# RWKV outputs of the first tile normalized on GpSimd during the second tile's rounds, roots and reciprocals tile by tile

## The chip, the cores and the metric

The kernel runs on one core of a Trainium2 chip. The metric is the device time of one execution in microseconds (us), median of the runs shown. The core has five engines that run their own instruction queues and meet only at semaphores: TensorE (PE; its weight loads are listed apart as PEld), VectorE (DVE), ScalarE (ACT), GpSimd (POOL) and SyncE (SP), which here only issues DMAs.

## The reference

Two transformer blocks on 256 tokens of width 2048. The change lies in the first one, in its mixer: an RWKV-7 group of 16 heads of 64 columns, whose outputs y are normalized head by head and then scaled, shifted, given a bonus and gated, and a sparse attention group that scores all keys with 16 small index heads, keeps the 64 best keys of a token and attends to them. Both halves, side by side, are the input of the product with `w_mix_out`.

```python
def rwkv7_group(p, mu, w0, w_decay_up, a0, a_up, g_up, k_k, k_a, r_k, lnx_w, lnx_b):
...
    _, y = lax.scan(step, s0, (tm(r4), tm(w4), tm(k4), tm(v4), tm(kk), tm(a4)))
    y = tm(y)
    mean = jnp.mean(y, axis=-1, keepdims=True)
    var = jnp.mean(jnp.square(y - mean), axis=-1, keepdims=True)
    yn = ((y - mean) * lax.rsqrt(var + RWKV_LN_EPS)).reshape(B, S, RWKV_WIDTH)
    yn = yn * lnx_w.astype(f32) + lnx_b.astype(f32)
    bonus = (jnp.sum(r4 * k4 * r_k.astype(f32), axis=-1, keepdims=True) * v4).reshape(B, S, RWKV_WIDTH)
    return ((yn + bonus) * g.astype(f32)).astype(p.dtype)

def dsa_group(p, pos):
...
        rel = jax.nn.relu(jnp.einsum('bqhd,bsd->bqhs', qib.astype(f32), ki))
        score = jnp.einsum('bqhs,bqh->bqs', rel, wib)
        causal = key_pos[None, :] <= q_pos[:, None]
        score = jnp.where(causal[None], score, -1e30)
        _, idx = lax.top_k(score, n_sel)
...
def first_block(...):
...
        p = rms_norm(h, norm_mix[l]) @ w_in[l]
        y_rwkv = rwkv7_group(p[..., :RWKV_COLS], ...)
        y_att = dsa_group(p[..., RWKV_COLS:], positions)
        h = h + jnp.concatenate([y_rwkv, y_att], axis=-1) @ w_mix_out[l]
...
```

## The kernel before

The 256 tokens are two tiles (`TILES`, index `t`) of 128 partitions. Products with weights run in fp32 split in a high and a low part: ScalarE rounds a slab of weights (L781), GpSimd makes its remainder (`rests`, L616), TensorE multiplies (L2014, L2024). After the input product `in` come three stages without weights, and then the product `mix`.

**RWKV rounds.** `PAIRS` holds four rounds: two for the first tile (n = 0, 1) and two for the second (n = 2, 3). A round is a chain of 16 stages between TensorE (L2142 to L2267), VectorE (L1508 to L1554) and ScalarE (L995 to L1018), for two groups `u` of four heads that alternate. A round starts with transposes (L2185) that VectorE and ScalarE copy out of PSUM (L1511, L997); then VectorE masks the products (L1514 to L1519; of these only L1517 reads two SBUF tiles, the others PSUM), and it ends with VectorE's L1552 and L1553, which write y over `key_t`. L1547, late in a round, reads two SBUF tiles too.

**Statistics and outputs of y.** GpSimd waits for both rounds of a tile (L694, L695) and makes the head means (L697, L698), the centred y (L699), its squares (L700), their head sums (L659, L661) and the variance plus epsilon (L702, which raises `s_yv`). This runs for tile 0 during round n = 2 and for tile 1 behind round n = 3. The root (ScalarE, L1034) and the reciprocal (VectorE, L1573) are taken once, for both tiles, on `yst[:, 1]`, 32 columns. Then GpSimd, from L704 on, runs the outputs of both tiles, six instructions of 128x1024 each: times the reciprocal root (L707), times and plus the gains (L708, L709), the bonus (L710), its addition (L711), the gate (L712, which raises `s_yr`). Right behind them in its queue stand the remainders of `mix` (L616), of which three can run before TensorE has used any.

**Index scores and the search.** After the rounds TensorE makes index products (L2297), ScalarE their relu (L1038), and VectorE adds sixteen of them, weighted, to the score of a tile: one copy (L1559) and sixteen L1564 of 128x128 for tile 0, of 128x256 for tile 1, each on two SBUF tiles and a column of scalars. The search takes eight pairs of L1576 and L1577, and two instructions turn the result into a mask (L1580, L1581). All of this stands in one VectorE queue, tile 0 before tile 1. `m` counts the index products, eight for a tile; the root stands in ScalarE's queue at m = 14, the reciprocal in VectorE's behind the last L1564.

**Attention and the turn.** `attend` (TensorE L2301, VectorE L1583, ScalarE L1042) runs eight units behind the masks; its VectorE instructions are L1606 and L1608, and L1597 and L1598 at the end of a unit. TensorE then waits for all of them (`a_done`, L2351) and for both `s_yr` (L2352), and transposes the mixed block (L2044). The product `mix` follows.

No planner sets the order here: it is the written order of each engine's queue, with semaphores between them.

Of the kernel before, what the change touches and what calls it, by code (L numbers as in the profile page):

```python
# [10 lines left out]
ACT = mybir.ActivationFunctionType  # L11
# [6 lines left out]
TILES = SEQ // P  # L18
# [4 lines left out]
R_W, R_HEAD = 1024, 64  # L23
# [91 lines left out]
def build(nc, A, out):  # L115
    with ExitStack() as ctx:
# [112 lines left out]
        key_t = at(z, TILES, R_W); z += TILES * R_W  # L229
# [362 lines left out]
        def _(pool):  # L592
# [100 lines left out]
            for t in range(TILES):  # L693
# [9 lines left out]
                pool.wait_ge(s_yv, t + 1)  # L703
            pool.wait_ge(s_ysd, 1)  # L704
            for t in range(TILES):
                y = key_t[:, t]
                step(TT(heads(y), heads(y), bc(yst[:, 1, t]), ALU.mult))  # L707
                step(TT(y, y, lnx[:, 0], ALU.mult))  # L708
                step(TT(y, y, lnx[:, 1], ALU.add))  # L709
                step(TT(heads(y_sq), heads(p[:, t, 2 * R_W:3 * R_W]), bc(bonus[:, t]), ALU.mult))  # L710
                step(TT(y, y, y_sq, ALU.add))  # L711
                TT(y, y, gate[:, t], ALU.mult).then_inc(s_yr, 1)  # L712
# [42 lines left out]
        def _(act):  # L755
# [237 lines left out]


            for n, (t, q) in enumerate(PAIRS):  # L995
                def copy(dst, b):
                    return act.activation(dst, b, ACT.Copy)  # L997
# [25 lines left out]
            for t in range(TILES):  # L1023
# [5 lines left out]
                for i in range(I_HEADS // 2):  # L1029
                    m = t * (I_HEADS // 2) + i  # L1030
                    if m == 14:

                        act.wait_ge(s_yv, TILES)
                        act.activation(yst[:, 1], yst[:, 1], ACT.Sqrt).then_inc(s_yr0, 1)  # L1034
                    act.wait_ge(s_ix, m + 1)
# [263 lines left out]
        def _(dve):  # L1299
# [205 lines left out]
            def pair_of(u, m):  # L1505

                return acc[:, 4 * u:4 * u + 2, m * P:(m + 1) * P].rearrange("p e (h c) -> p e h c", h=2)
            for n, (t, q) in enumerate(PAIRS):  # L1508
                for u in range(2):
                    g_wait(dve, n, "turned", u, 0)  # L1510
                    dve.tensor_copy(S_(u, 0), bank(4 * u + 2)).then_inc(g_ve, 1)  # L1511
# [44 lines left out]
            for t in range(TILES):  # L1556
                nk = (t + 1) * P
                sc = score[:, t, 0:nk]
                step(dve.tensor_copy(sc, causal[:, t, META:META + nk]))  # L1559
                for i in range(I_HEADS // 2):  # L1560
# [8 lines left out]
                    dve.wait_ge(s_acc2, m + 1)  # L1569
                if t == TILES - 1:  # L1570

                    dve.wait_ge(s_yr0, 1)
                    dve.reciprocal(yst[:, 1], yst[:, 1]).then_inc(s_ysd, 1)  # L1573
                src = sc
# [1024 lines left out]
```

## Time and profile before

| | |
|---|---|
| median of 3 runs | 3416.51 us (3412.78 to 3419.33) |
| the profiled execution | 3420.07 us, its span 3417.9 us |
| busy: PE, DVE, ACT, POOL | 2502.5, 1777.3, 1081.6, 2365.1 us |
| RWKV rounds (about) | 385 to 517 us from the span's start |
| scores and search, both tiles | 516 to 558 us |
| sparse attention | 558 to 576 us |
| turn of the mixed block | 576.50 us |

The profile is of one execution, so its times within the span are set against 3420.07, not against the median. Shares of the whole span say little here, for the change lies in a stretch of some 100 us; the timelines of that stretch are the views to read. A row of a timeline is its start, its length, the engine, the line, the operation with the tiles written and read (`lasting` and `zone` are the two parts of SBUF, `acc` is PSUM), the shape, and in brackets the idle time of the engine before it with what ended it.

### The profile page before, as it was taken

The numbers are of one execution on the slowest core, as the hardware profiler recorded it, in microseconds if no ns is written. First come the engines' busy times: TensorE is split into PE (matmuls) and PEld (weight loads), VectorE is DVE, ScalarE is ACT, GpSimd is POOL, SyncE is SP. The second block draws the span as 40 slices with busy tenths as digits, with TensorE's granted clock in tenths as the row PEclk, the third lists the DMA queues.
The fourth block names the chain that finished last, engine by engine and source line by source line (L and its number), as shares of the span: only waits on it lengthen the run. The fifth ranks groups of instructions, "written<-read, shape, count | busy, mean of one in ns | idle before, by whom it ended". The sixth has DMA issues, their size and how long they took to land.

```text
span 3417.9 us, 42238 instructions
## 1 busy us (share of the span) xinstructions
PE 2502.5 (73%) x15833; PEld 1974.4 (58%) x15833; DVE 1777.3 (52%) x2456; ACT 1081.6 (32%) x2108; POOL 2365.1 (69%) x1677
## 2 busy tenths in 40 slices
PE   6999996989999999989999999007602730571077
PEld 5777885789988998889987679003201310230022
DVE  4375656243200222220412446887797879788954
ACT  6444324564444445454546554000000000000000
POOL 7400316869999999987866579885687578567852
PEclk9999998999999999999999999559856975796589
DMA  5675300546655665555544355999999999999998
GB/s 179 206 236 148 100 3 32 178 126 185 189 187 189 179 189 180 190 155 156 162 125 134 105 166 186 378 427 427 427 427 428 427 427 428 427 426 427 427 427 343
DMA packets 241376, 868.10 MB, mean 254 GB/s; under 512 B 18940, under 2 KB 21484, under 8 KB 174886
## 3 DMA queue, kind: packets, MB, share of 16 engines
q0 software_dynamic: 73776, 536.97, 37.3%
q1 hardware_dynamic: 163414, 316.11, 30.5%
q10 hardware_dynamic: 4016, 12.75, 1.2%
q8 instruction: 106, 1.74, 0.2%
q14 instruction: 64, 0.52, 0.0%
HBM read 860.24 MB, written 2.10 MB: 252 GB/s over the span
## 4 chain that ended last, share of the span: by engine, by line
PE 50%; POOL 18%; DMA 12%; DVE 7%; issue 4%; ACT 1%; DVEq 0%; ACTq 0%; POOLq 0%; SPq 0%
PE acc L2014 19%; PE acc L2024 19%; DMA zone<-in_peer_v,zone 11%; POOL zone L736 9%; POOL lasting L736 9%; PE acc L2020 3%; PE acc L2152 3%; PE acc L2578 2%; DVE lasting L1955 1%; DMA lasting<-in_peer_u,zone 1%; PE acc L2467 1%; POOL w_lo L616 1%; DVE zone L1564 0%; PE acc L2061 0%; PE acc L2185 0%
## 5 line engine op out<-in xcount | busy, mean ns | idle before, releaser
L616 POOL TENSOR_TENSOR w_lo<-lasting,w_hi 128x512 fp32r<-128x512 f32 x1024 | 1372.5, 1360 | 283.7 <-ACT w_hi L781 264.7
L781 ACT ACTIVATE w_hi<-lasting 128x512 fp32r<-128x512 f32 (+1 forms) x1184 | 741.5, 631 | 902.4 <-PE acc L2014 456.7
L2578 PE MATMUL acc<-zone,lasting 128*128 128x512 f32 x512 | 251.1, 647 | 708.4 <-ACT lasting L1293 647.1
L2578 PEld LDWEIGHTS acc<-zone,lasting 128*128 128x128 f32 x512 | 103.7, 208 | 855.1 <-ACT lasting L1293 502.7
L2024 PE MATMUL acc<-x_hi,w_hi 128*128 128x256 f32 (+1 forms) x1856 | 305.7, 287 | 14.8 <-POOL w_lo L616 5.6
L1925 DVE CUSTOM_DVE_ANT_0 zone<-lasting,zone 128x2048 f32<-128x2048 f32 x128 | 293.6, 2294 | 34.2 <-DMA lasting<-in_peer_u,zone 24.7
L736 POOL DMA_INDIRECT zone<-in_peer_v,zone x128 | 189.1, 1477 | 174.1 <-DVE lasting L1955 74.6
L1925 DVE CUSTOM_DVE_ANT_0 zone<-zone 128x2048 f32<-128x2048 f32 x128 | 293.4, 2292 | 22.5 <-DMA zone<-in_peer_u,zone 13.3
L2024 PE MATMUL acc<-x_lo,w_hi 128*128 128x256 f32 (+1 forms) x1856 | 298.9, 283 | 0.0
L2024 PE MATMUL acc<-x_hi,w_lo 128*128 128x256 f32 (+1 forms) x1856 | 298.8, 283 | 0.0
L736 POOL DMA_INDIRECT zone<-in_peer_u,zone x128 | 262.6, 2052 | 46.7 <-issue 37.5
L2578 PE MATMUL acc<-lasting 128*128 128x512 f32 x512 | 241.9, 628 | 62.0 <-DMA lasting<-in_peer_v,zone 60.7
L736 POOL DMA_INDIRECT lasting<-in_peer_u,zone x128 | 240.5, 1879 | 57.1 <-issue 37.5
L2024 PEld LDWEIGHTS acc<-x_hi,w_hi 128*128 128x128 f32 x1856 | 255.4, 189 | 22.6 <-POOL w_lo L616 8.7
L2024 PEld LDWEIGHTS acc<-x_lo,w_hi 128*128 128x128 f32 x1856 | 255.5, 189 | 0.0
L2024 PEld LDWEIGHTS acc<-x_hi,w_lo 128*128 128x128 f32 x1856 | 255.0, 189 | 0.0
L736 POOL DMA_INDIRECT lasting<-in_peer_v,zone x128 | 206.0, 1610 | 68.3 <-issue 34.7
L1285 ACT ACTIVATE zone<-zone 128x64 f32<-128x64 f32 x4 | 1.0, 256 | 749.8 <-DVEq L1929 749.8
L2014 PE MATMUL acc<-w_hi,x_hi 128*128 128x512 f32 (+1 forms) x672 | 216.3, 403 | 19.3 <-DVE w_lo L1375 8.6
L2578 PEld LDWEIGHTS acc<-lasting 128*128 128x128 f32 x512 | 100.4, 200 | 202.9 <-issue 191.8
L2014 PE MATMUL acc<-w_hi,x_lo 128*128 128x512 f32 (+1 forms) x672 | 210.8, 395 | 0.0
L2014 PE MATMUL acc<-w_lo,x_hi 128*128 128x512 f32 (+1 forms) x672 | 209.1, 392 | 0.0
(419 smaller groups left out, 3945.3 us busy)
## 6 DMA issues: line engine op xcount, KB each, us to landing
lasting<-in_w_in SPq DMA_DIRECT2D x200, 512.0 KB, 3.7
lasting<-in_w_up SPq DMA_DIRECT2D x128, 512.0 KB, 3.8
lasting<-in_w_down SPq DMA_DIRECT2D x128, 512.0 KB, 4.3
lasting<-in_w_mix_out SPq DMA_DIRECT2D x32, 512.0 KB, 3.6
lasting<-in_w_out SPq DMA_DIRECT2D x32, 512.0 KB, 3.6
lasting<-in_peer_w_query SPq DMA_DIRECT2D x32, 512.0 KB, 3.6
lasting<-in_w_kv_cross SPq DMA_DIRECT2D x16, 512.0 KB, 3.8
lasting<-in_w_q_cross SPq DMA_DIRECT2D x8, 512.0 KB, 3.6
```

The source lines that it names most:

```text
L616: pool.tensor_tensor(w_lo[:, k, 0:width], ring[:, slot, s % SLOT_SLABS, 0:width], w_hi[:, k, 0:width].bitcast(FP32), ALU.subtract).then_in ...
L736: pool.indirect_dma_start(out=rows_buf[2 * n + k], out_offset=None, in_=A[table][0], in_offset=bass.IndirectOffsetOnAxis(ap=experts[:, hx ...
L781: act.activation(w_hi[:, s % PARTS, 0:width], ring[:, slot, s % SLOT_SLABS, 0:width], ACT.Copy).then_inc(hi_ready, 1)
L1285: act.activation(part, part, ACT.Gelu).then_inc(s_gelu, 1)
L1925: last = dve.tensor_tensor_reduce(out=junk, in0=rows_buf[2 * n + k], in1=hb[:, t], scale=1.0, scalar=0.0, op0=ALU.mult, op1=ALU.add, accum ...
L1955: last = STT(h[:, t], rows_buf[2 * n + k], coef[:, t, slot:slot + 1], h[:, t], ALU.mult, ALU.add)
L2014: last = pe.matmul(bank(banks[t])[:, 0:width], xp[:, s, g.lo + t * P:g.lo + (t + 1) * P], wp[:, k, 0:width], **kw)
L2020: last = pe.matmul(bank(banks[f // 2])[:, f % 2 * SEQ:(f % 2 + 1) * SEQ], wp[:, k, f * P:(f + 1) * P], xp[:, s, g.lo:g.hi], skip_group_che ...
L2024: last = pe.matmul(bank(banks[f])[:, 0:g.hi - g.lo], wp[:, k, f * P:(f + 1) * P], xp[:, s, g.lo:g.hi], **kw)
L2152: return pe.matmul(out, lhsT, rhs, start=start, stop=stop, skip_group_check=check)
L2467: last = pe.matmul(two_out(m), probT2[0:size, m % 2, n * P:(n + 1) * P], v, start=n == 0, stop=n == t + 1)
L2578: last = pe.matmul(bank(4 * t + c), diag[:, n // 2, k], rows_buf[2 * n + k][:, c * CHUNK:(c + 1) * CHUNK], start=hx % 2 == 0 and i == 0 an ...
```

## The change

GpSimd now runs all of a tile's work in one pass: the statistics of tile 0, its six outputs, then the statistics of tile 1 and its six outputs. The six of tile 0 wait for a root and a reciprocal of their own (16 columns). Its root stands in ScalarE's queue between rounds n = 2 and n = 3, its reciprocal at the head of round n = 3 in VectorE's queue. For tile 1 the root stands before the relu m = 8, and the reciprocal at the head of tile 1's scores, before the copy and the sixteen additions. The bonus of tile 0 goes through `early_sq`, since the place of `y_sq` is used by the rounds.

```diff
--- before.py
+++ after.py
@@ -701,14 +701,13 @@
                 step(head_sums(yst[:, 1, t], heads(early_sq), early_sq))
                 pool.tensor_scalar(yst[:, 1, t], yst[:, 1, t], 1.0 / R_HEAD, 64e-5, ALU.mult, ALU.add).then_inc(s_yv, 1)
                 pool.wait_ge(s_yv, t + 1)
-            pool.wait_ge(s_ysd, 1)
-            for t in range(TILES):
-                y = key_t[:, t]
+                pool.wait_ge(s_ysd, t + 1)
                 step(TT(heads(y), heads(y), bc(yst[:, 1, t]), ALU.mult))
                 step(TT(y, y, lnx[:, 0], ALU.mult))
                 step(TT(y, y, lnx[:, 1], ALU.add))
-                step(TT(heads(y_sq), heads(p[:, t, 2 * R_W:3 * R_W]), bc(bonus[:, t]), ALU.mult))
-                step(TT(y, y, y_sq, ALU.add))
+                bonus_y = (early_sq, y_sq)[t]
+                step(TT(heads(bonus_y), heads(p[:, t, 2 * R_W:3 * R_W]), bc(bonus[:, t]), ALU.mult))
+                step(TT(y, y, bonus_y, ALU.add))
                 TT(y, y, gate[:, t], ALU.mult).then_inc(s_yr, 1)
 
             pool.wait_ge(lo_ready, G["mix"].slab(0, 0, 0))
@@ -992,7 +991,14 @@
             act.dma_start(lnx[:, 1], A["lnx_b"][0].partition_broadcast(P)).then_inc(s_lnx, 16)
 
 
+            def root_y(t):
+                act.wait_ge(s_yv, t + 1)
+                act.activation(yst[:, 1, t], yst[:, 1, t], ACT.Sqrt).then_inc(s_yr0, 1)
+
             for n, (t, q) in enumerate(PAIRS):
+                if n == 3:
+                    root_y(0)
+
                 def copy(dst, b):
                     return act.activation(dst, b, ACT.Copy)
                 for u in range(2):
@@ -1028,10 +1034,8 @@
                 nk = (t + 1) * P
                 for i in range(I_HEADS // 2):
                     m = t * (I_HEADS // 2) + i
-                    if m == 14:
-
-                        act.wait_ge(s_yv, TILES)
-                        act.activation(yst[:, 1], yst[:, 1], ACT.Sqrt).then_inc(s_yr0, 1)
+                    if m == 8:
+                        root_y(1)
                     act.wait_ge(s_ix, m + 1)
                     if m >= 4:
                         act.wait_ge(s_acc2, m - 3)
@@ -1506,6 +1510,9 @@
 
                 return acc[:, 4 * u:4 * u + 2, m * P:(m + 1) * P].rearrange("p e (h c) -> p e h c", h=2)
             for n, (t, q) in enumerate(PAIRS):
+                if n == 3:
+                    dve.wait_ge(s_yr0, 1)
+                    dve.reciprocal(yst[:, 1, 0], yst[:, 1, 0]).then_inc(s_ysd, 1)
                 for u in range(2):
                     g_wait(dve, n, "turned", u, 0)
                     dve.tensor_copy(S_(u, 0), bank(4 * u + 2)).then_inc(g_ve, 1)
@@ -1556,6 +1563,9 @@
             for t in range(TILES):
                 nk = (t + 1) * P
                 sc = score[:, t, 0:nk]
+                if t == 1:
+                    dve.wait_ge(s_yr0, 2)
+                    dve.reciprocal(yst[:, 1, 1], yst[:, 1, 1]).then_inc(s_ysd, 1)
                 step(dve.tensor_copy(sc, causal[:, t, META:META + nk]))
                 for i in range(I_HEADS // 2):
                     m = t * (I_HEADS // 2) + i
@@ -1567,10 +1577,6 @@
                             step(last)
                     last.then_inc(s_acc2, 1)
                     dve.wait_ge(s_acc2, m + 1)
-                if t == TILES - 1:
-
-                    dve.wait_ge(s_yr0, 1)
-                    dve.reciprocal(yst[:, 1], yst[:, 1]).then_inc(s_ysd, 1)
                 src = sc
                 for r in range(TOPK // 8):
                     step(dve.max(m8, src))
```

GpSimd's queue behind the variance of tile 0, before: the statistics of tile 1 come next.

```order
L661 TENSOR_TENSOR lasting<-zone 128x16
L702 TENSOR_SCALAR lasting<-lasting 128x16
L659 TENSOR_TENSOR zone<-zone 128x16x32
L659 TENSOR_TENSOR zone<-zone 128x16x16
L659 TENSOR_TENSOR zone<-zone 128x16x8
```

The same place after (line numbers of the changed kernel):

```order
L702 TENSOR_SCALAR lasting<-lasting 128x16
L705 TENSOR_TENSOR zone<-zone,lasting 128x1024
L706 TENSOR_TENSOR zone<-zone,lasting 128x1024
L707 TENSOR_TENSOR zone<-zone,lasting 128x1024
L709 TENSOR_TENSOR zone<-zone,lasting 128x1024
L710 TENSOR_TENSOR zone<-zone 128x1024
L711 TENSOR_TENSOR zone<-zone 128x1024
L659 TENSOR_TENSOR zone<-zone 128x16x32
```

The six outputs of tile 0 have moved ahead of the statistics of tile 1; the six of tile 1 stand right behind their own statistics.

VectorE's queue around the scores of tile 1, before:

```order
L1580 TENSOR_SCALAR zone<-zone 128x128
L1581 TENSOR_TENSOR zone<-zone,lasting 128x128
L1559 COPY zone<-lasting 128x256
L1564 SCALAR_TENSOR_TENSOR zone<-lasting,zone 128x256 x16
L1573 RECIPROCAL lasting<-lasting 128x32
```

And after:

```order
L1586 TENSOR_SCALAR zone<-zone 128x128
L1587 TENSOR_TENSOR zone<-zone,lasting 128x128
L1568 RECIPROCAL lasting<-lasting 128x16
L1569 COPY zone<-lasting 128x256
L1574 SCALAR_TENSOR_TENSOR zone<-lasting,zone 128x256 x16
```

The reciprocal that releases GpSimd's outputs of tile 1 has moved from behind the sixteen additions to ahead of them, between tile 0's mask and tile 1's copy.

## Rows read from the trace of the kernel before

**Rows 1.** Timeline, VectorE and TensorE, at the turn.

```profile
576.02 0.42 DVE L1598 TENSOR_TENSOR zone<-acc,lasting 128x256 f32<-128x256 f32 x1
...
576.50 4.52 PE L2044 MATMUL acc<-lasting,zone 128*128 128x128 f32 x32 [0.72 <-DVE zone L1598]
```

**Rows 2.** Timeline of GpSimd, 547 to 578.

```profile
547.23 1.90 POOL L707 TENSOR_TENSOR zone<-zone,lasting 128x1024 f32<-128x1024 f32 x1 [18.57 <-DVE lasting L1573]
...
554.05 1.90 POOL L710 TENSOR_TENSOR lasting<-zone,lasting 128x1024 f32<-128x1024 f32 x1
...
556.03 2.34 POOL L711 TENSOR_TENSOR zone<-zone,lasting 128x1024 f32<-128x1024 f32 x1
...
574.41 3.73 POOL L616 TENSOR_TENSOR w_lo<-lasting,w_hi 128x512 fp32r<-128x512 f32 x3
```

**Rows 3.** Timeline of VectorE, second tile's scores, search and masks.

```profile
538.06 0.29 DVE L1559 COPY zone<-lasting 128x256 f32<-128x256 f32 x1
...
538.39 8.30 DVE L1564 SCALAR_TENSOR_TENSOR zone<-lasting,zone 128x256 f32<-128x256 f32 x16
...
546.73 0.35 DVE L1573 RECIPROCAL lasting<-lasting 128x32 f32<-128x32 f32 x1
...
547.00 0.37 DVE L1576 MAX8 lasting<-zone 128x8 f32<-128x256 f32 x1
...
554.82 1.28 DVE L1580 TENSOR_SCALAR zone<-zone 128x256 f32<-128x256 f32 x1
...
556.13 2.52 DVE L1581 TENSOR_TENSOR zone<-zone,lasting 128x256 f32<-128x256 f32 x1
...
558.68 0.42 DVE L1606 TENSOR_TENSOR zone<-acc,zone 128x256 f32<-128x256 f32 x1
```

**Rows 4.** L1517 (count, shortest/median/longest ns, starts), timelines of rounds.

```profile
L1517 DVE TENSOR_TENSOR lasting<-lasting x4: 415/415/454, 390.3 to 487.8; 128x256 f32<-128x256 f32 x4
...
L1517 DVE TENSOR_TENSOR zone<-zone,lasting x4: 415/446/974, 392.5 to 490.0; 128x256 f32<-128x256 f32 x4
...
457.06 0.97 DVE L1517 TENSOR_TENSOR zone<-zone,lasting 128x256 f32<-128x256 f32 x1
...
455.85 1.90 POOL L699 TENSOR_TENSOR zone<-zone,lasting 128x1024 f32<-128x1024 f32 x1
...
419.54 0.69 DVE L1511 COPY lasting<-acc 128x512 f32<-128x512 f32 x1 [0.46 <-PE acc L2185]
...
451.81 0.69 DVE L1511 COPY lasting<-acc 128x512 f32<-128x512 f32 x1 [0.46 <-PE acc L2185]
...
484.71 0.69 DVE L1511 COPY lasting<-acc 128x512 f32<-128x512 f32 x1 [0.46 <-PE acc L2185]
...
484.71 0.60 ACT L997 ACTIVATE lasting<-acc 128x512 f32<-128x512 f32 x1 [8.08 <-PE acc L2185]
```

**Rows 5.** L1564 by line; timelines of VectorE, GpSimd, ScalarE, first scores.

```profile
L1564 DVE SCALAR_TENSOR_TENSOR zone<-lasting,zone x1: 1864/1864/1864, 522.9 to 522.9; 128x128 f32<-128x128 f32 x1
...
522.51 0.35 DVE L1564 SCALAR_TENSOR_TENSOR zone<-lasting,zone 128x128 f32<-128x128 f32 x1 [5.86 <-ACT lasting L1038]
...
524.80 1.30 DVE L1564 SCALAR_TENSOR_TENSOR zone<-lasting,zone 128x128 f32<-128x128 f32 x1
...
522.73 1.89 POOL L700 TENSOR_TENSOR zone<-zone 128x1024 f32<-128x1024 f32 x1
...
524.70 1.26 POOL L659 TENSOR_TENSOR zone<-zone 128x512 f32<-128x512 f32 x1
...
534.25 1.08 ACT L1038 ACTIVATE lasting<-acc 128x512 f32<-128x512 f32 x2 [0.84 <-PE acc L2297]
```

**Rows 6.** By line: L1655 on VectorE, beside GpSimd's L616 in the products.

```profile
L1655 DVE TENSOR_TENSOR lasting<-lasting,zone x4: 692/1619/1624, 1348.8 to 1482.0; 128x512 f32<-128x512 f32 x4
```

**Rows 7.** By windows: busy of PE, PEld, DVE, ACT, POOL, granted clock, DMA.

```profile
546.00:565.00 19.00, 5.10 (x20) 4.34 (x20) 15.78 (x39) 4.07 (x18) 17.30 (x8) 0.50 0.00 0
...
565.00:583.00 18.00, 14.98 (x109) 12.82 (x107) 13.88 (x30) 12.03 (x31) 13.58 (x9) 0.99 0.09 30
```

## The prediction

> **What bounds the kernel now.** I read first who releases TensorE at the end of the sparse attention, since everything the change moves is needed there: the turn of the mixed block waits for VectorE's last output (`a_done`) and for GpSimd's two normalized tiles (`s_yr`). In the timelines VectorE's last multiply starts at 576.02 and takes 0.42, and the turn starts at 576.50 [rows 1]; GpSimd ended its twelve output instructions by 574.41, when it took up the next product's remainders [rows 2]. So GpSimd is 2.0 us early and VectorE ends this stage. Taking GpSimd's work out of the tail gives nothing by itself; it pays or costs only through what it does to VectorE.
>
> It does do something. At 554.82 a TENSOR_SCALAR of 128x256 takes 1.28 us and at 556.13 a TENSOR_TENSOR of 128x256 takes 2.52 [rows 3], where a copy of the same shape takes 0.29 [rows 3] and a multiply or add of two SBUF tiles of 128x256 takes 0.415 [rows 4]. Set beside GpSimd's timeline: its L710 ends at 554.05 + 1.90 = 555.95 and VectorE's instruction at 556.10; its L711 ends at 556.03 + 2.34 = 558.37 and VectorE's at 558.65 [rows 2, 3]. VectorE's instruction ends 0.15 to 0.28 after GpSimd's: it was held for the whole of it. The same pattern stands twice more. In the third round a L1517 starting at 457.06 takes 0.97 and ends 0.28 after GpSimd's L699 (455.85 + 1.90 = 457.75) [rows 4], and that round is 32.90 us long against 32.27 for the one before (484.71 - 451.81 and 451.81 - 419.54) [rows 4], so 0.56 of waiting became 0.63 of the chain. In the first tile's scores, a L1564 of 128x128 that starts at 522.9 takes 1.86, and the next one 1.30, each ending 0.14 or so after one GpSimd instruction (522.73 + 1.89 = 524.62; 524.70 + 1.26 = 525.96) [rows 5]. One GpSimd instruction lets one such VectorE instruction through. Not held are instructions that read PSUM, and the search for the largest scores: its sixteen instructions run from 547.00 to 554.82, 0.49 each, with GpSimd busy all along [rows 2, 3].
>
> **The change, part by part.** Against the profiled execution.
>
> *Roots on ScalarE.* The first now comes after the third round's last copy. ScalarE is idle 8.08 us before its first copy of the fourth round [rows 4]; a table load and one activation on 16 columns fit many times over. The second comes before the relu that waits for TensorE 0.84 us anyway [rows 5], and VectorE uses that relu's result only from 538.39 on [rows 3]. Cost 0. If this cover were gone, a few tenths.
>
> *Reciprocals on VectorE.* The 128x32 one at 546.73 took 0.27 of the queue [rows 3]; in its place stand two of 128x16. The one before the fourth round falls into the 0.46 us in which VectorE waits for the transposes [rows 4]. The other stands ahead of the second tile's scores: 0.27 goes there and comes back behind them. Sum 0. Queued behind it is the whole score chain, but its root is made some 4 us earlier.
>
> *First tile's six outputs in the fourth round.* GpSimd starts 0.50 after the reciprocal (547.23 - 546.73) [rows 2, 3]. VectorE is free at 484.71 - 0.46 = 484.25, so GpSimd starts at about 484.7. Its first instruction takes 1.90 with 0.08 behind it, like L710; the second and third come 2.42 apart ((554.05 - 547.23 - 1.98) / 2) [rows 2], so they end at 489.05 and 491.45. The round's two L1517 started at 487.8 and 490.0 [rows 4]. The first falls into GpSimd's second instruction and ends at 489.05 + 0.28 = 489.33 in place of 488.2: +1.1. The second, pushed to 491.1, ends at 491.73 in place of 491.5: +0.3. The round's other instructions on two SBUF tiles (L1547) come after GpSimd's 498.3. **+1.4**, with bounds of 0 (both miss) and 4.8 (each meets a whole one); I take 1.4, since the starts are rows. All of it lies on the path, as in the third round.
>
> *Second tile's six outputs at the second tile's scores.* They were held back until 547.23, behind the scores; now they go from 0.50 after the reciprocal that stands at the head of them. Call the head T (538.06 before). GpSimd's block of six takes (574.41 - 547.23) / 2 = 13.59, and right behind it come three remainders for the next product, 3.73, whose inputs are ready [rows 2]: nine instructions, 17.3 us, until T + 17.8. In the same time stand VectorE's sixteen L1564 of 128x256, each on two SBUF tiles, which took 8.30 together, 0.519 each, while GpSimd was idle [rows 2, 3]. At one per GpSimd instruction nine of them take until T + 17.8 + 0.28 = T + 18.1, and the other seven 3.6: T + 21.7. Before, the search for the largest scores began at 547.00 = T + 8.9 [rows 3]. **+12.8**. The bounds are 0 (if L1564 at this width is not held) and 14.6 (if GpSimd is delayed too, below). I take 12.8, as the nearest rows are the same instruction at half the width. That the remainders hold as well is shown by L1655: 0.69 alone, 1.62 beside them [rows 6].
>
> *The tail.* GpSimd is then idle when the masks are made: 1.28 goes to 0.29 and 2.52 to 0.415. **-3.1**, bounds -3.1 and 0. What is late next is VectorE still: the attention behind it (558.68 to 576.44) [rows 1, 3] reads PSUM, and I leave it as long as it was.
>
> Sum: 1.4 + 12.8 - 3.1 = +11.1. Behind the turn the products run TensorE-bound, so the shift stays. The profiled execution took 3420.07, to which this gives 3431.2; it stands 3.56 above the median of the runs shown, so the median becomes 3416.51 + 11.1 = **3427.6**.
>
> **A rule beside the rows.** In the rows GpSimd loses nothing: the 128x512 instruction that ran beside held ones took 1.26 and began 0.08 after the one before [rows 5], and VectorE's held instruction had 0.14 to 0.28 left when GpSimd's next began. The Trainium skill, SBUF — State Buffer, Who interferes with whom, says that a VectorE instruction with two SBUF inputs and a GpSimd one that reads SBUF share one pair of ports, and that whoever issues first keeps it for the whole instruction while the other is fully blocked. By that, GpSimd would be late too each time.
>
> **Rivals.**
> 1. *Both wait in turn.* Each of the nine GpSimd instructions also waits for the 0.2 us that VectorE's still runs: 9 x 0.2 = +1.8, 3429.4. For it: both use the same memory. Against it: [rows 5] show no gap. The rule above gives this. Chance 0.10.
> 2. *Held only in part.* If an L1564 of 128x256 pays on average half of a GpSimd instruction, or slips two through at a time, the 12.8 is 6.4, the sum +4.7: 3421.2. For it: the overlap was seen only for a few instructions. Chance 0.12.
> 3. *Not slower: GpSimd gives way.* If the sixteen L1564 keep their 0.519, because VectorE's queue gets in first and GpSimd pays, then what is left is the tail: 1.4 - 3.1 = -1.7, 3414.8 (3413.4 if the fourth round pays nothing as well). It decides at the first L1564 behind the second reciprocal: 0.49 or about 2 us long. For it: the very first L1564 at 522.51 took 0.35 beside GpSimd [rows 5], though GpSimd's instruction was about to end. Chance 0.13.
> 4. *A cold TensorE.* TensorE's granted clock is 0.50 from 546 to 565, after an idle stretch, and 0.99 from 565 to 583 [rows 7]. Its idle stretch grows by some 10 us. If the rise came later by as much again, the attention's 15.0 us of TensorE work there would in part run at 1.2 GHz: +5, 3432.6. Chance 0.07.
>
> That the change does not do what it says needs a late first reciprocal; ScalarE's 8.08 us of slack exclude it.
>
> **How the numbers follow.** The forecast, 3427.6, has 0.58. The range should leave out no more than 2 in 10: from 3419.0, below rival 2, to 3434.0, over rival 4; it leaves out rival 3 and some tails. A difference under 0.2%, 6.8 us, can't be told from none here. Slower by more: the forecast, rivals 1 and 4, and a third of rival 2, 0.79. Within: rival 3, without the corner in which it also saves elsewhere, and the rest of rival 2, 0.19. Faster by more: nothing on GpSimd bounds a stretch of 6.8 us, 0.02.
>
> **What would show it.** In the trace after: L1564's second-tile form with a mean near 1.3 us in place of 0.49, nine of them of 1.5 to 2.6; the search beginning some 21.7 us after the second reciprocal; the fourth round at 33.7 us; the masks at 0.3 and 0.4; the turn of the mixed block at about 587.6 with GpSimd long done. The prediction is wrong if the sixteen stay at 8.3 us together, or if GpSimd's six outputs take clearly more than 13.6 us.

## The result and the profile after

The changed kernel takes 3427.61 us (median of 7 runs, 3422.96 to 3431.20) against 3416.51 of the kernel before (7 runs, 3412.78 to 3425.94): a ratio of 1.0030, with a 95% interval of 1.0021 to 1.0039, or 7 to 13 us more. The profiled execution took 3431.20 with a span of 3429.4; before it was 3417.9.

Timelines of the fourth round after the change: VectorE, then GpSimd.

```profile
483.37 0.24 DVE L1515 RECIPROCAL lasting<-lasting 128x16 f32<-128x16 f32 x1
483.91 0.69 DVE L1518 COPY lasting<-acc 128x512 f32<-128x512 f32 x1 [0.30 <-PE acc L2191]
...
487.04 1.34 DVE L1524 TENSOR_TENSOR lasting<-lasting 128x256 f32<-128x256 f32 x1
...
490.08 0.80 DVE L1524 TENSOR_TENSOR zone<-zone,lasting 128x256 f32<-128x256 f32 x1
...
516.59 0.42 DVE L1560 TENSOR_TENSOR zone<-acc,zone 128x256 f32<-128x256 f32 x1
...
483.76 1.90 POOL L705 TENSOR_TENSOR zone<-zone,lasting 128x1024 f32<-128x1024 f32 x1 [20.77 <-DVE lasting L1515]
485.74 2.36 POOL L706 TENSOR_TENSOR zone<-zone,lasting 128x1024 f32<-128x1024 f32 x1
488.18 2.42 POOL L707 TENSOR_TENSOR zone<-zone,lasting 128x1024 f32<-128x1024 f32 x1
```

GpSimd starts the first tile's outputs at 483.76, 0.39 behind the start of the reciprocal. VectorE's L1524 (L1517 before) at 487.04 ends with GpSimd's second instruction (485.74 + 2.36 = 488.10) plus 0.28, and the one at 490.08 ends 0.28 behind the third (488.18 + 2.42 = 490.60). They took 1.34 and 0.80 where 0.415 is the length alone [rows 4]. From its first copy (483.91) to the end of its last addition the round is 33.1 us; the last addition starts 32.68 after the copy, against 31.39 in the trace before.

Timelines of the second tile's scores, search and masks: VectorE, GpSimd, and TensorE's turn of the mixed block.

```profile
538.55 0.25 DVE L1568 RECIPROCAL lasting<-lasting 128x16 f32<-128x16 f32 x1
...
538.99 21.97 DVE L1574 SCALAR_TENSOR_TENSOR zone<-lasting,zone 128x256 f32<-128x256 f32 x16
561.00 0.43 DVE L1582 MAX8 lasting<-zone 128x8 f32<-128x256 f32 x1
...
568.87 0.29 DVE L1586 TENSOR_SCALAR zone<-zone 128x256 f32<-128x256 f32 x1
569.20 0.42 DVE L1587 TENSOR_TENSOR zone<-zone,lasting 128x256 f32<-128x256 f32 x1
569.65 0.42 DVE L1612 TENSOR_TENSOR zone<-acc,zone 128x256 f32<-128x256 f32 x1
...
538.96 1.90 POOL L705 TENSOR_TENSOR zone<-zone,lasting 128x1024 f32<-128x1024 f32 x1 [9.81 <-DVE lasting L1568]
...
552.79 4.25 POOL L616 TENSOR_TENSOR w_lo<-lasting,w_hi 128x512 fp32r<-128x512 f32 x3
...
587.71 4.52 PE L2050 MATMUL acc<-lasting,zone 128*128 128x128 f32 x32 [0.72 <-DVE zone L1604]
```

The sixteen additions take 21.97 us in place of 8.30 [rows 3]. The search begins 561.00 - 538.55 = 22.45 behind the head (the reciprocal's start), where it began 547.00 - 538.06 = 8.94 behind the head (the copy's start) before [rows 3]: +13.5. The masks take 0.78 until L1612 starts, in place of 3.86 [rows 3]: -3.1. GpSimd is done with the outputs at 552.8 and with the three remainders at 557.04, without a wait; the turn waits for VectorE alone, at 587.71 in place of 576.50 [rows 1].

The sixteen additions in three stretches of time; the columns are the count, then the shortest, median and longest of one in ns, and the first and last start.

```profile
L1574 DVE SCALAR_TENSOR_TENSOR zone<-lasting,zone x6: 2007/2444/2451, 539.0 to 550.7; 128x256 f32<-128x256 f32 x6
...
L1574 DVE SCALAR_TENSOR_TENSOR zone<-lasting,zone x3: 1366/1368/1370, 553.1 to 555.9; 128x256 f32<-128x256 f32 x3
...
L1574 DVE SCALAR_TENSOR_TENSOR zone<-lasting,zone x7: 484/485/485, 557.4 to 560.5; 128x256 f32<-128x256 f32 x7
```

Six additions run beside GpSimd's six outputs and take 2.0 to 2.45 us, three run beside its three remainders and take 1.37, and the seven behind them take 0.485. Each of the nine ends with one of GpSimd's instructions, plus 0.28.

### The profile page after: what moved, and what is told of

It reads as the page before. It is cut to its first block, busy times and chain, and to the rows that moved or that the text cites. A ratio compares the mean times of both kernels' runs of the same rounds, so it can differ in the third digit from the quotient of the medians.

```text
span 3429.4 us, 42241 instructions
## 1 busy us (share of the span) xinstructions
PE 2507.9 (73%) x15833; PEld 1973.9 (58%) x15833; DVE 1788.3 (52%) x2457; ACT 1081.6 (32%) x2109; POOL 2364.7 (69%) x1677
## 4 chain that ended last, share of the span: by engine, by line
PE 51%; POOL 18%; DMA 12%; DVE 7%; issue 4%; ACT 1%; DVEq 0%; ACTq 0%; POOLq 0%
PE acc L2020 20%; PE acc L2030 19%; DMA zone<-in_peer_v,zone 10%; POOL zone L735 9%; POOL lasting L735 9%; PE acc L2026 3%; PE acc L2158 3%; PE acc L2584 2%; DVE lasting L1961 1%; DMA zone<-in_peer_u,zone 1%; DVE zone L1574 1%; PE acc L2473 1%; POOL w_lo L616 1%; DMA lasting<-in_peer_v,zone 1%; PE acc L2067 0%
## 5 line engine op out<-in xcount | busy, mean ns | idle before, releaser
L616 POOL TENSOR_TENSOR w_lo<-lasting,w_hi 128x512 fp32r<-128x512 f32 x1024 | 1374.3, 1361 | 314.1 <-ACT w_hi L780 294.3
L1931 DVE CUSTOM_DVE_ANT_0 zone<-lasting,zone 128x2048 f32<-128x2048 f32 x128 | 293.4, 2292 | 33.7 <-DMA lasting<-in_peer_u,zone 24.0
L1931 DVE CUSTOM_DVE_ANT_0 zone<-zone 128x2048 f32<-128x2048 f32 x128 | 293.4, 2292 | 22.7 <-DMA zone<-in_peer_u,zone 13.5
```

Of the source, the lines that this page charges most:

```text
L616: pool.tensor_tensor(w_lo[:, k, 0:width], ring[:, slot, s % SLOT_SLABS, 0:width], w_hi[:, k, 0:width].bitcast(FP32), ALU.subtract).then_in ...
L1931: last = dve.tensor_tensor_reduce(out=junk, in0=rows_buf[2 * n + k], in1=hb[:, t], scale=1.0, scalar=0.0, op0=ALU.mult, op1=ALU.add, accum ...
```

## The experiments

A measure that needs no median: in each trace, the time from the fourth round's first copy to the turn of the mixed block. It holds every stage in which the change moved an instruction; the start of the product behind the turn is looked at by itself, under the programs run again. The ratios given with the experiments are against executions of the kernel before that were taken beside the experiment (medians 3416.30 us for the first four, 3415.43 for those that follow), not against the 3416.51 above.

| kernel | copy to turn, us | against before |
|---|---|---|
| before (first, second profile) | 91.79, 91.55 | |
| after (first, second, third profile) | 103.80, 103.90, 103.54 | +12.0 |
| second reciprocal behind the additions | 92.91 | +1.1 |
| all twelve outputs beside the additions | 113.24 | +21.5 |
| second tile's scores in PSUM | 90.39 | -1.4 |
| remainders wait for the masks | 101.99 | +10.2 |
| sixteen memsets | 92.67 | +0.9 |
| first reciprocal later in its round | 101.75 | +10.0 |
| all holds removed, new order | 86.17 | -5.6 |
| all holds removed, old order | 87.12 | -4.7 |

The theory is that of the prediction: VectorE's instructions on two SBUF tiles wait, one for one, for GpSimd's instructions. The rivals are that the roots, reciprocals or their waits cost the time, or TensorE's clock.

### The second reciprocal behind the additions

```diff
-                if t == 1:
-                    dve.wait_ge(s_yr0, 2)
-                    dve.reciprocal(yst[:, 1, 1], yst[:, 1, 1]).then_inc(s_ysd, 1)
                 step(dve.tensor_copy(sc, causal[:, t, META:META + nk]))
...
+                if t == 1:
+                    dve.wait_ge(s_yr0, 2)
+                    dve.reciprocal(yst[:, 1, 1], yst[:, 1, 1]).then_inc(s_ysd, 1)
                 src = sc
```

> The changed kernel with one part undone: the second tile's reciprocal stands again behind the sixteen score additions, so GpSimd's six outputs of that tile start only then; the first tile's part stays in the fourth round. Theory (VectorE's instructions on two SBUF tiles are held one by one by GpSimd's): the sixteen additions take 8.3 us together as before, not 21.97; the fourth round keeps its +1.3; the masks are held again (3.9 us for both against 0.8), since GpSimd's six run from the reciprocal on for 13.6; sum +1.3 us against the kernel before, within 0.2%. Rival A (the loss comes from the roots and reciprocals, two table uses, or the waits on them): still some +11 us. Rival B (TensorE's clock): the slow start of the mix product stays, +2 to +3 us.

Measured: 3418.74 us (10 runs), ratio to before 1.0007, interval 0.9997 to 1.0017. Timeline of VectorE, and one stretch of the fourth round by windows (busy of PE, PEld, DVE, ACT, POOL, granted clock, DMA share, GB/s).

```profile
539.44 8.30 DVE L1571 SCALAR_TENSOR_TENSOR zone<-lasting,zone 128x256 f32<-128x256 f32 x16
...
555.77 1.28 DVE L1586 TENSOR_SCALAR zone<-zone 128x256 f32<-128x256 f32 x1
557.08 2.51 DVE L1587 TENSOR_TENSOR zone<-zone,lasting 128x256 f32<-128x256 f32 x1
...
487.76:491.76 4.00, 2.81 (x68) 2.81 (x70) 3.60 (x9) 0.00 (x0) 3.84 (x3) 0.68 0.00 0
```

The additions are back at 8.30, the masks at 1.28 and 2.51. Moving one instruction of 0.25 us by eight microseconds makes and unmakes the loss, so it is neither the roots nor the number of reciprocals. The fourth round is 0.7 longer here than in the changed kernel: in this execution TensorE's granted clock was 0.68 over 4 us of it, where it was 1.00 in the changed kernel. The +1.1 is thus +2.0 in the round and -0.8 in the attention behind, which was shorter in this execution; more on both below. The sum foreseen was +1.3. That +1.1 comes near it is in part chance, since these two deviations nearly cancel; both are small beside the 11 us in question.

### All twelve outputs beside the additions

The kernel before, with its one reciprocal at the head of the second tile's scores, and the root that it needs at m = 8 in ScalarE's queue, where the changed kernel has its second one.

```diff
-                    if m == 14:
+                    if m == 8:
...
                 sc = score[:, t, 0:nk]
+                if t == TILES - 1:
+                    dve.wait_ge(s_yr0, 1)
+                    dve.reciprocal(yst[:, 1], yst[:, 1]).then_inc(s_ysd, 1)
...
-                if t == TILES - 1:
-
-                    dve.wait_ge(s_yr0, 1)
-                    dve.reciprocal(yst[:, 1], yst[:, 1]).then_inc(s_ysd, 1)
```

> The kernel before, with the one reciprocal of both tiles moved to the head of the second tile's scores (and the root to m = 8): GpSimd has twelve output instructions and three remainders to run beside the sixteen additions, in place of six and three. Theory: fifteen of the sixteen are held, 0.5 + 27.2 + 3.7 + 0.3 = 31.7 us, the last takes 0.5: the search begins some 32.2 us after the reciprocal (8.9 before, 22.4 in the changed kernel), so +23 there, -3.1 at the masks, nothing in the fourth round: about +20 us against before, +0.6%. Rival (a fixed cost of the earlier reciprocal, or only a partial hold that has run out): about the +11 of the changed kernel or less.

Measured: 3437.68 us (4 runs), ratio 1.0062, interval 1.0045 to 1.0079. Timeline of VectorE.

```profile
538.64 0.35 DVE L1561 RECIPROCAL lasting<-lasting 128x32 f32<-128x32 f32 x1
...
539.18 32.85 DVE L1567 SCALAR_TENSOR_TENSOR zone<-lasting,zone 128x256 f32<-128x256 f32 x16
572.06 0.43 DVE L1575 MAX8 lasting<-zone 128x8 f32<-128x256 f32 x1
```

With fifteen of GpSimd's instructions beside sixteen additions the search begins 33.4 behind the head, 32.2 expected. The 1.2 more is GpSimd's: its fifteen instructions took 32.1 (539.15 to 571.22) and not the 30.9 put in. The loss grows with GpSimd's instructions, not with the reciprocal: +24.5 at the search for fifteen, +13.5 for nine.

### The second tile's scores in PSUM

The changed kernel; GpSimd's work and its times stay.

```diff
-                sc = score[:, t, 0:nk]
+                sc = score[:, t, 0:nk] if t == 0 else bank(5)[:, 0:nk]
```

> The changed kernel with the second tile's scores kept in PSUM, so that each of its sixteen additions has one SBUF tile and one PSUM tile as inputs, and GpSimd's work beside it stays as it is. Theory (only two SBUF tiles are held): the sixteen take about 8.3 us together; the search begins about 9 us after the reciprocal; the masks then meet the last of GpSimd's nine instructions, at 17 to 18 us after the reciprocal, and lose up to 2; sum against before: +1.3 for the fourth round, -1 to -3 for the masks: -2 to 0 us. Rival (GpSimd slows VectorE whatever it reads, or the queue waits for something else): the sixteen stay near 22 us and the sum at +11.

Measured: 3416.67 us (10 runs), ratio 0.9999, interval 0.9989 to 1.0008. Timelines of VectorE and GpSimd.

```profile
538.68 8.36 DVE L1574 SCALAR_TENSOR_TENSOR acc<-lasting,zone,acc 128x256 f32<-128x256 f32 x16
547.07 0.43 DVE L1582 MAX8 lasting<-acc 128x8 f32<-128x256 f32 x1
...
554.96 0.90 DVE L1586 TENSOR_SCALAR zone<-zone 128x256 f32<-128x256 f32 x1
555.90 0.43 DVE L1587 TENSOR_TENSOR zone<-zone,lasting 128x256 f32<-128x256 f32 x1
...
552.00 3.71 POOL L616 TENSOR_TENSOR w_lo<-lasting,w_hi 128x512 fp32r<-128x512 f32 x3
```

This one separates best. The same sixteen additions, beside the same nine GpSimd instructions (538.47 to 555.71), take 8.36 once one of their two inputs lies in PSUM. The 11 us are gone. As expected the mask, still from SBUF to SBUF, meets the last remainder and takes 0.90 in place of 0.29; it ends at 555.86, 0.15 behind it.

### The remainders wait

The changed kernel; GpSimd's first three remainders wait until VectorE is past the second tile's masks.

```diff
             pool.wait_ge(lo_ready, G["mix"].slab(0, 0, 0))
+            pool.wait_ge(a_sm, 1)
             rests("mix", "cross_q", "cross_o", "up0", "down0", "up1", "down1")
```

> The changed kernel in which GpSimd's first three remainders of the mix product wait until the second tile's masks are made; nothing else is moved. Theory: six additions are held in place of nine, about 0.5 + 13.6 + 0.3 + 10 x 0.52 = 19.6 us from the reciprocal to the search, against 22.4: -2.9 us against the changed kernel, +8.3 against before. The three remainders then run beside the attention, which reads PSUM, at no cost. Rival (the remainders do not hold): no change against the changed kernel. Rival B (the earlier remainders help the mix product): slower than that.

Measured: 3423.75 us (7 runs), ratio 1.0031, interval 1.0019 to 1.0042. Timeline of VectorE.

```profile
537.58 0.25 DVE L1569 RECIPROCAL lasting<-lasting 128x16 f32<-128x16 f32 x1
...
538.02 19.33 DVE L1575 SCALAR_TENSOR_TENSOR zone<-lasting,zone 128x256 f32<-128x256 f32 x16
557.38 0.43 DVE L1583 MAX8 lasting<-zone 128x8 f32<-128x256 f32 x1
```

The search begins 557.38 - 537.58 = 19.8 behind the head, 19.6 expected, and 2.65 sooner than in the changed kernel: the three remainders hold too. At the turn 1.8 us of this are left (101.99 against 103.80), as the fourth round of this execution had such a dip of the clock as in the first experiment (0.76 over 4 us) and was 0.8 longer. The times of whole runs do not show it: the ratio to before is 1.0031 here and 1.0030 for the changed kernel.

### Memsets in place of reads

The kernel before, with sixteen memsets in the time in which GpSimd would wait.

```diff
+            pool.wait_ge(s_acc2, 8)
+            for k in range(16):
+                step(pool.memset(y_sq, 0.0))
             pool.wait_ge(s_ysd, 1)
```

> The kernel before, with sixteen GpSimd memsets of 128x1024 (into y_sq, which is dead there) put in from the end of the first tile's scores on, while GpSimd would wait; they only write SBUF. Question: is VectorE held by any GpSimd instruction, or only by those that read SBUF? If only by those that read: the sixteen additions that fall beside the memsets take 0.485 each as before, 8.3 us together. If by any: each addition beside a memset ends with it, at the length of a memset. The outputs behind the memsets may start later than before (at most a few us), which is then seen at the turn and is no part of the question.

Measured: 3420.26 us (one run, beside 3415.43 of before). Timelines of VectorE and GpSimd.

```profile
537.25 0.42 DVE L1583 TENSOR_SCALAR zone<-zone 128x128 f32<-128x128 f32 x1
...
538.03 0.72 DVE L1562 COPY zone<-lasting 128x256 f32<-128x256 f32 x1
538.78 8.30 DVE L1567 SCALAR_TENSOR_TENSOR zone<-lasting,zone 128x256 f32<-128x256 f32 x16
...
531.59 16.10 POOL L706 MEMSET lasting<- 128x1024 f32 x16 [3.16 <-DVE zone L1567]
```

The memsets fill GpSimd from 531.59 to 547.69, one a microsecond, and the additions in that time take 8.30. So neither GpSimd's being busy nor its writing holds them; what a memset lacks beside the outputs is the reading of SBUF. But two instructions with a single SBUF input are held a little: the first tile's mask took 0.42, where it was 0.23 in every other trace, and the copy of 128x256 took 0.72 in place of 0.29 [rows 3]. They end about 0.1 us behind the end of a memset each. There are two kinds of hold, then: instructions on two SBUF tiles are held by GpSimd's instructions that read, and these copy and TENSOR_SCALAR forms by its memsets too. The second kind rests on these two instructions of one execution; that a TENSOR_SCALAR on one tile is held beside GpSimd's outputs also stands in [rows 3] (1.28). The Trainium skill, SBUF — State Buffer, Who interferes with whom, draws the same line: two SBUF inputs of VectorE contend with a GpSimd instruction that reads SBUF and not with one that only writes it, and the two-port modes, which copy and tensor_scalar can enter, contend with GpSimd in general. The 8.30 beside memsets, the 21.97 beside reads and the two held instructions agree with it.

### The first reciprocal later in its round

```diff
             for n, (t, q) in enumerate(PAIRS):
-                if n == 3:
-                    dve.wait_ge(s_yr0, 1)
-                    dve.reciprocal(yst[:, 1, 0], yst[:, 1, 0]).then_inc(s_ysd, 1)
                 for u in range(2):
                     g_wait(dve, n, "turned", u, 0)
...
+                if n == 3:
+                    dve.wait_ge(s_yr0, 1)
+                    dve.reciprocal(yst[:, 1, 0], yst[:, 1, 0]).then_inc(s_ysd, 1)
                 for u in range(2):
                     g_wait(dve, n, "square", u, 0)
```

> The changed kernel with the first tile's reciprocal moved within the fourth round, from its head to behind the masks of the pairs (L1517 included), so that GpSimd's six outputs start some 6 us later and end some 1 us before the first L1547. Theory: the two L1517 of that round take 0.415 again, the round 31.4 us from its first copy to its last addition in place of 32.7, -1.3 us against the changed kernel. Rival (the round grew because of the reciprocal in VectorE's queue or the root in ScalarE's): the reciprocal now stands between masks and products with no idle time over it, so the round is as long as or longer than 32.7.

Measured: 3420.11 us (one run; single runs of the changed kernel spread over 3419 to 3431, so the trace has to tell). By line, with the last of the four starts in the fourth round:

```profile
L1521 DVE TENSOR_TENSOR lasting<-lasting x4: 414/415/415, 387.5 to 485.3; 128x256 f32<-128x256 f32 x4
L1521 DVE TENSOR_TENSOR zone<-zone,lasting x4: 415/415/975, 389.6 to 487.4; 128x256 f32<-128x256 f32 x4
```

Both L1521 of the fourth round (485.3 and 487.4) are at 0.415; the 0.975 is the third round's, which the statistics hold as before. The last addition starts 31.37 behind the first copy, as in the kernel before (31.39), against 32.68. So the whole +1.3 came from these two instructions, and six outputs of a tile do fit into the round at no cost, if they start behind the masks of the pairs.

### All holds removed

The changed kernel with the reciprocal as just shown, the scores of both tiles in PSUM, and the second tile's mask made by way of that bank. A wait of TensorE keeps the bank free until the first tile's scores have been read.

```diff
-                sc = score[:, t, 0:nk]
+                sc = bank(5)[:, 0:nk]
+                dve.wait_ge(s_qT2, t + 1)
...
                     src = left[:, 0:nk]
+                    if t == 0 and r == 0:
+                        dve.sem_inc(s_sel, 1)
                 un = unsel[:, t, 0:nk]
-                step(TS(un, left[:, 0:nk], TAKEN / 2, NEG, ALU.is_gt, ALU.mult))
-                step(TT(un, un, causal[:, t, META:META + nk], ALU.add))
+                flags = un if t == 0 else sc
+                step(TS(flags, left[:, 0:nk], TAKEN / 2, NEG, ALU.is_gt, ALU.mult))
+                step(TT(un, flags, causal[:, t, META:META + nk], ALU.add))
...
                     for i in range(8):
+                        if t and k == 4 and i == 4:
+                            pe.wait_ge(s_sel, 1)
                         last = pe.transpose(bank(k + i // 4)[:, (i % 4) * P:(i % 4 + 1) * P],
```

> The changed kernel with all three holds taken away: the first tile's reciprocal behind the pairs' masks, the scores of both tiles in a PSUM bank (TensorE's last four query transposes of the second tile wait for the first tile's first search step), and the second tile's mask made by way of that bank. Theory: fourth round +0, first tile's scores 9.2 to about 6.2 (-3.0, unless the delayed transposes come late: up to +1), second tile's scores 8.3, masks -3.0: about -5 to -6 us against before, faster by 0.15 to 0.18%. Rival (the wait moves on, to GpSimd's outputs or to the transposes): -2 to 0.

Measured: 3411.22 us (11 runs, 3400.25 to 3413.50), ratio to before 0.9981, interval 0.9971 to 0.9992: faster than the kernel before by 0.1 to 0.3%. Timelines of VectorE, GpSimd and TensorE.

```profile
520.75 6.23 DVE L1575 SCALAR_TENSOR_TENSOR acc<-lasting,zone,acc 128x128 f32<-128x128 f32 x16 [0.84 <-ACT lasting L1042]
...
534.07 8.37 DVE L1575 SCALAR_TENSOR_TENSOR acc<-lasting,zone,acc 128x256 f32<-128x256 f32 x16
...
550.35 0.43 DVE L1590 TENSOR_SCALAR acc<-zone 128x256 f32<-128x256 f32 x1
...
550.81 0.42 DVE L1591 TENSOR_TENSOR zone<-acc,lasting 128x256 f32<-128x256 f32 x1
...
533.86 1.90 POOL L705 TENSOR_TENSOR zone<-zone,lasting 128x1024 f32<-128x1024 f32 x1 [7.04 <-DVE lasting L1569]
...
547.40 3.72 POOL L616 TENSOR_TENSOR w_lo<-lasting,w_hi 128x512 fp32r<-128x512 f32 x3
...
569.14 4.52 PE L2054 MATMUL acc<-lasting,zone 128*128 128x128 f32 x32 [0.72 <-DVE zone L1608]
```

The first tile's additions take 6.23 in place of 9.18, the second's 8.37, the masks 0.43 and 0.42, and the turn comes 5.6 us earlier. GpSimd's nine instructions, undisturbed, take 551.12 - 533.86 = 17.26.

The same on the kernel before, GpSimd's order untouched:

> The kernel before with the PSUM scores and the PSUM mask alone, GpSimd's order untouched: it tells what the tile-by-tile order is worth once nothing on VectorE is held. Theory: VectorE's attention ends some 6 us earlier, but GpSimd's twelve outputs start with the reciprocal (3.0 earlier) and end at about 571.4, after VectorE's 570.4: the turn waits for GpSimd, -5 us against before, about 1 us behind the run that has the new order as well.

Measured: 3411.82 us (11 runs), ratio 0.9990, interval 0.9981 to 0.9999. Timelines of GpSimd and TensorE.

```profile
567.63 2.34 POOL L712 TENSOR_TENSOR zone<-zone 128x1024 f32<-128x1024 f32 x1
569.93 3.74 POOL L616 TENSOR_TENSOR w_lo<-lasting,w_hi 128x512 fp32r<-128x512 f32 x3
...
570.08 4.49 PE L2048 MATMUL acc<-lasting,zone 128*128 128x128 f32 x32 [1.66 <-DVE zone L1602]
```

Here GpSimd's last output (567.63 + 2.34 = 569.97) releases the turn at 570.08. The row names VectorE as the releaser, but VectorE had ended at 569.08, and the idle time before the turn is 1.66 in place of 0.72. The tile-by-tile order is worth 0.95 us at this point, by the traces; the medians cannot tell the two kernels apart.

### Two programs again

The start of the mix product was slow in the changed kernel's first trace: by windows,

```profile
594.37:601.37 7.00, 7.00 (x24) 5.62 (x25) 0.00 (x0) 1.90 (x3) 3.24 (x4) 0.77 0.23 75
```

a granted clock of 0.77 in its first 7 us, where 583.17 to 590.17 had 1.00 before. The product's stretch in the chain of work grew from 89.24 to 90.70 us.

> The changed kernel once more, unaltered, for a second profiled execution. In the first one the mix product began at a granted clock of 0.77 for its first 7 us (1.22 us for its first two matmuls' pair, 0.73 in the kernel before), which cost about 1.5 us of the 11.5. Theory: this is of the execution, not of the change, since four of ten traces so far show it (the changed kernel, with the reciprocal behind the additions, with the remainders waiting, with PSUM scores) and six do not, without a pattern in what is changed; then it may come or not, and the additions stay at 21.97 us and the fourth round at 32.7 either way. Rival: the change makes it (later and colder TensorE); then it is here again, and in the kernel before it never is.

> The kernel before once more, unaltered. Theory: the product's start at a clock of 0.77 can come here too; all waits on VectorE are as in the first profile (additions 8.30, masks 1.28 and 2.52, fourth round 31.4). Rival: always at 1.00 here, as the change makes it.

> The changed kernel a third time, for the same question. Theory: the clock at the product's start varies between executions of one program; the rest is the same to 0.1 us.

Measured, timeline of VectorE and window of the product's start, second profile of the changed kernel:

```profile
538.85 21.98 DVE L1574 SCALAR_TENSOR_TENSOR zone<-lasting,zone 128x256 f32<-128x256 f32 x16
...
593.96:600.96 7.00, 7.00 (x30) 5.74 (x31) 0.00 (x0) 2.53 (x4) 4.69 (x5) 1.00 0.28 97
```

And third:

```profile
536.19 21.97 DVE L1574 SCALAR_TENSOR_TENSOR zone<-lasting,zone 128x256 f32<-128x256 f32 x16
...
591.30:598.30 7.00, 7.00 (x30) 5.74 (x31) 0.00 (x0) 2.53 (x4) 4.69 (x5) 1.00 0.31 95
```

Both start at 1.00, with the additions at 21.98 and 21.97. The second profile of the kernel before, 3414.42 us, has 8.29, 1.30 and 2.51, and its product starts at 1.00 as well. So the changed kernel does not always have the dip, and the rival that it always does has fallen. That the dip has nothing to do with the change is not shown: of the eight traces with the tile-by-tile order four have it (0.76 to 0.78), of the five with the old order none, and this part of the rival stands. It would be worth some 1.5 us in the executions that have it. (The other three that had it are those with the second reciprocal behind the additions, with the remainders waiting, and with all holds removed; the last is the one that the text on record calls "with PSUM scores". The one with the second tile's scores alone in PSUM started at 1.00.) The third execution also shows how little one time says: its span is 3417.4, 12 us below the first, while the same VectorE instruction (L1829), some 1300 us behind the turn, was reached only 2.9 earlier (1880.76 and 1883.68 in the chains). The rest arose between there and 2357 us, in the stretch in which the chain waits for the gathers of the experts: the first long one of these waits took 16.14 in place of 21.06, and from the next one on (2344.71 and 2356.76) the two are 12 apart. Why the gathers differ was not asked.

## Why the prediction was right, point by point

**What bounds the stage.** Right: the turn waited for VectorE before and after, and GpSimd's earlier end gave nothing.

**Roots and reciprocals, 0.** Right, to 0.2: the second reciprocal puts the additions 0.11 later behind the head, and the place behind them gives back 0.27. ScalarE idled 6.55 before its first copy of the round, behind the table load and the root, and the reciprocal of 0.24 left 0.30 of VectorE's wait.

**Fourth round, +1.4.** Measured +1.29. The two waits were foreseen as +1.1 and +0.3 and were +0.93 and +0.39, as GpSimd started 0.39 and not 0.50 behind the reciprocal. The 33.7 named as a sign is 32.27 + 1.4, the time from one round's first copy to the next round's, which the fourth round does not have; from its first copy to the start of its last addition it took 32.68, against 31.39. In two of the six traces with this hold the clock dip made the round 0.7 to 0.8 longer still, a term that the sum did not have (see the end).

**Scores, +12.8.** Measured +13.5. The count was right, nine held and seven free. The size was 0.7 short: GpSimd's nine instructions took 18.1 in place of 17.3. Rival 1 had the direction, that GpSimd waits as well, but at 0.2 each; against the 17.26 undisturbed it is 0.8 / 9 = 0.09 each. The three remainders lost most of it (4.25 in place of 3.73, and 3.72 undisturbed), some 0.17 each; the outputs lost 0.04 each. The prediction's reading that GpSimd loses nothing held for its rows of 128 columns, and not for these of 256.

**Masks, -3.1.** Measured -3.1.

**The attention behind, 0.** Measured +0.2: 18.06 from L1612 to the turn in place of 17.82. In the traces in which VectorE ended the stage the stretch was 17.0 to 18.1 long, and 17.82 and 17.81 in the other two profiles of the changed kernel. TensorE's granted clock rises from 0.50 within it, and not equally soon: in the window from 564 to 566 us it was 0.92 in the first experiment, where TensorE had taken up the attention at about 561.5, and 0.66 in the kernel before, where it had at about 560.5. So the +0.2 is taken as spread between executions.

**Sum.** +11.1 foreseen; the turn moved by +11.2 in the first pair of traces, of which 0.8 had been gained ahead of the fourth round by chance, so +12.0 from the round's first copy on; the medians differ by 11.1. That the median agrees to the tenth is luck: its interval is 6 us wide. What is shown is the mechanism: by the sixteen additions themselves, which take 21.97 beside GpSimd's reads, 8.30 beside its memsets and 8.36 beside the reads with one input in PSUM, and by the count, as fifteen of GpSimd's instructions cost more than nine.

**The rivals.** Held in part (2) and GpSimd giving way (3) fell with the 21.97. The cold TensorE (4) did not come in the attention: the clock rose within it as before, and the stretch was no more than 0.2 longer. Its price of 5 us was not paid; what the clock did take in single executions is 0.7 to 0.8 us in the fourth round and 1.5 at the product's start.

## What to carry to other kernels

Before work is moved to GpSimd "beside" VectorE, look at what VectorE runs there: an instruction on two SBUF tiles waits for the end of the GpSimd instruction that runs and reads SBUF, however short it is itself, so sixteen short additions beside nine long ones cost 13.5 us to gain 3. The sign is in the profile of the kernel before: a VectorE instruction of several times its usual length that ends 0.1 to 0.3 us behind one of GpSimd's. The cure can be as small as the place of one operand: an accumulator in PSUM made the hold vanish (8.36 in place of 21.97), and with both tiles' scores and the second mask by way of PSUM, and the first reciprocal behind the masks of the pairs, the same order of GpSimd's work went from 0.3% slower to 0.2% faster than the kernel before. Of the 5.6 us by which the turn came earlier, 4.7 are had with the old order too, and 0.95 come from the order.

## What was not expected of the hardware

GpSimd pays too when it holds VectorE. Beside the additions of 256 columns it is little, 0.09 us an instruction. That it need not be little stands in the trace of the kernel before, beside the L1655 of 512 columns that took 1.62 [rows 6]. By line, the remainders of a long stretch before it, and as a timeline the one that begins while L1655 still runs (it ends at 1350.41):

```profile
L616 POOL TENSOR_TENSOR w_lo<-lasting,w_hi x101: 1278/1298/2282, 1199.3 to 1339.5; 128x512 fp32r<-128x512 f32 x101
...
1349.82 1.73 POOL L616 TENSOR_TENSOR w_lo<-lasting,w_hi 128x512 fp32r<-128x512 f32 x1
```

This remainder takes 1.73 where the median of the 101 is 1.30: 0.43 more. So GpSimd's loss was nothing beside 128 columns (1.26 [rows 5]), 0.04 to 0.17 beside 256 and 0.43 beside 512. No experiment varied the width alone.

GpSimd's memsets hold VectorE's copy and TENSOR_SCALAR from SBUF to SBUF (0.72 in place of 0.29, 0.42 in place of 0.23) though not its additions on two SBUF tiles.

A hold on VectorE can reach TensorE's clock. Timelines of TensorE in the fourth round, kernel before and changed kernel:

```profile
488.97 0.69 PE L2152 MATMUL acc<-lasting 64*64 64x64 f32 x24 [1.40 <-DVE lasting L1519]
...
489.10 0.69 PE L2158 MATMUL acc<-lasting 64*64 64x64 f32 x24 [2.33 <-DVE lasting L1526]
```

The held L1524 makes TensorE's idle time behind the pairs 2.33 in place of 1.40. In two of the six traces with the 2.33 the granted clock fell from 1.00 there (0.68 and 0.76 over the 4 us around its end), and the round took 0.7 to 0.8 longer; in the other four, with the same idle time, and in the seven with the shorter one it stayed at 1.00. The start of the mix product, behind an idle time of 2.15 in the changed kernel's first trace, was at 0.76 to 0.78 in four of thirteen traces. Why it falls in one execution and not in the next stays open.
